# A hybrid encoder step on one core: the vector engine's part of a pair's first half is placed one slot behind the other engines' part

## What is computed

```python
h = rmsnorm(x, g_mix)
z = h @ w_in                                     # 1024 x 2048
ya, v_rows = gmlp_mix(gelu(z[..., :1024]), g_v, w_s, b_s)
xc, conv = causal_conv(z[..., 1024:1536], conv_buf, conv_w, conv_b)
yb, lru = rg_lru(xc, h0, w_a, b_a, w_i, b_i, lam)   # gates, then a scan over time
yb = yb * gelu(z[..., 1536:])
x = x + concat([rmsnorm(ya, g_out_a), rmsnorm(yb, g_out_b)]) @ w_out
# 8 heads x 16 experts for each token, out of 16384
q = rmsnorm(x, g_ffn) @ w_q
top-16 sums over two sets of 128 sub-keys -> expert numbers and softmax weights g
x = x + sum_k g_k * gelu(u_tab[e_k] . h2) * v_tab[e_k]
y = rmsnorm(x, g_final)
```

## Time and profile before

| | |
|---|---|
| median of 3 runs | 1813.78 us (1809.45 to 1820.84) |
| the profiled execution | 1812.19 us, its span 1810.4 us |
| busy share of the span: PE, DVE, ACT, POOL | 81%, 79%, 35%, 44% |
| mean granted clock of TensorE | 0.905 of full speed |
| chain that ended last, by engine | PE 31%, DMA 28%, DVE 16%, issue 9%, POOL 8%, ACT 7% |

### The profile page before, as it was taken

The page is one execution under the profiler, slowest core; times in us unless marked ns, Lnnn a source line. Parts: engine busy times, 40 slices in busy tenths (PEclk is TensorE's granted clock), DMA queues, the critical chain, the costliest instruction groups (busy, mean ns, idle before and its releaser), DMA issues.

```text
span 1810.4 us, 16904 instructions
## 1 busy us (share of the span) xinstructions
PE 1461.9 (81%) x4706; PEld 793.1 (44%) x4706; DVE 1426.9 (79%) x3039; ACT 634.1 (35%) x1935; POOL 796.1 (44%) x667
## 2 busy tenths in 40 slices
PE   6799796667675652876869988999998788899997
PEld 5485343433342212534735655433334455433332
DVE  1278688999898879689998999996668988766665
ACT  4335534232222221420147876221115666311112
POOL 2023234476777667758834444222223445322220
PEclk9899898877887786988979999999998988999999
DMA  9489999999999999989988989999998999999996
GB/s 351 155 332 409 388 354 385 339 399 412 394 400 408 384 415 403 389 313 403 380 308 319 357 331 379 417 417 417 417 417 340 375 343 348 409 417 417 417 417 254
DMA packets 146478, 675.75 MB, mean 373 GB/s; under 512 B 15216, under 2 KB 15472, under 8 KB 97232
## 3 DMA queue, kind: packets, MB, share of 16 engines
q0 software_dynamic: 92832, 538.39, 75.5%
q1 hardware_dynamic: 50496, 132.68, 19.0%
q10 hardware_dynamic: 3056, 3.61, 0.6%
HBM read 671.61 MB, written 3.01 MB: 373 GB/s over the span
## 4 chain that ended last, share of the span: by engine, by line
PE 31%; DMA 28%; DVE 16%; issue 9%; POOL 8%; ACT 7%; ACTq 0%; DVEq 0%; POOLq 0%; SPq 0%
DMA arena<-experts 19%; PE accY L1493 9%; DMA ring<-experts,idc 8%; PE pb L1478 8%; POOL ring L620 7%; PE pb L1298 4%; DVE ring L920 3%; DVE ring L909 3%; PE pb L1467 3%; PE pb L1307 2%; ACT arena L1223 2%; PE pq L1424 2%; DVE arena L969 1%; PE pb L1316 1%; POOL ring L618 1%
## 5 line engine op out<-in xcount | busy, mean ns | idle before, releaser
L618 POOL DMA_INDIRECT ring<-experts,idc x384 | 457.6, 1192 | 856.9 <-DVE xt L929 386.1
L909 DVE CUSTOM_DVE_ANT_0 ring<-ring,h 128x1024 f32<-128x1024 f32 x384 | 466.2, 1221 | 197.6 <-DMA ring<-experts,idc 196.4
L1493 PE MATMUL accY<-ring,diag 128*128 128x512 f32 x792 | 456.5, 713 | 200.4 <-ACT diag L1209 200.4
L1478 PE MATMUL pb<-arena 128*128 128x512 f32 x1024 | 473.6, 607 | 19.1 <-DMA arena<-experts 12.3
L620 POOL DMA_INDIRECT ring<-experts,idc x256 | 328.3, 1283 | 112.3 <-issue 76.9
L1198 ACT ACTIVATE ge<-zt 128x1 f32<-128x1 f32 x384 | 76.4, 199 | 771.6 <-DVE zt L909 770.4
L1493 PEld LDWEIGHTS accY<-ring,diag 128*128 128x128 f32 x792 | 161.5, 221 | 410.5 <-ACT diag L1209 271.9
L1478 PEld LDWEIGHTS pb<-arena 128*128 128x128 f32 x1024 | 186.2, 191 | 304.9 <-issue 195.0
L929 DVE SCALAR_TENSOR_TENSOR xt<-ring,coef,xt 128x1024 f32<-128x1024 f32 x186 | 238.1, 1280 | 7.5 <-ACT coef L1202 7.4
L1424 PE MATMUL pq<-arena 128*128 128x256 f32 (+1 forms) x768 | 152.5, 358 | 9.0 <-ACT arena L1193 4.7
L920 DVE CUSTOM_DVE_ANT_0 ring<-ring,arena 128x1024 f32<-128x1024 f32 x128 | 153.4, 1221 | 7.0 <-DMA ring<-experts,idc 6.1
(11 more groups left out here) (178 smaller groups left out, 1082.7 us busy)
## 6 DMA issues: line engine op xcount, KB each, us to landing
arena<-experts SPq DMA_DIRECT2D x128, 512.0 KB, 15.1
arena<-w_q SPq DMA_DIRECT2D x12, 2048.0 KB, 18.2
arena<-w_in SPq DMA_DIRECT2D x11, 2048.0 KB, 21.4
ring<-experts,idc POOLq DMA_INDIRECT x640, 9.3
arena<-w_out SPq DMA_DIRECT2D x4, 2048.0 KB, 20.7
ring<-w_out SPq DMA_DIRECT2D x2, 2048.0 KB, 20.3
xt<-x_all SPq DMA_DIRECT2D x5, 512.0 KB, 13.5
y_all<-xt ACTq DMA_DIRECT2D x5, 512.0 KB, 3.5
```

The costliest lines, as they stand in the source:

```text
L618: nc.gpsimd.indirect_dma_start(ring[:, at // 2], None, experts, index).then_inc(gat[at], 16)
L909: V.tensor_tensor_reduce(out=half(g), in0=half(g), in1=h2[:], scale=1.0, scalar=0.0, op0=ALU.mult, op1=ALU.add, accum_out=zt[:, s % 8:s % ...
L1478: ins = T.matmul(pb[:, 2 * j + k], cm[:, i, j * P:(j + 1) * P], vring[:, n % VRING, k * 512:(k + 1) * 512], start=i == 0, stop=i == BLOCKS ...
L1493: ins = T.matmul(accY[:, j], diag[:, (n - 1) % DIAGS], ring[:, place, D + j * 512:D + (j + 1) * 512], start=first, stop=final)
```

## The change

A second kind of item, `"Iv"`, stands for DVE's part of a step. It is due 1.2 us of the imagined schedule behind the step in the first pair and 0.8 us in the second; a step of the first pair is due every 2.2 us there, one of the second every 1.5 us. DVE acts on `"Iv"` in place of `"I"`; the other engines act on `"I"` as before. In the first tile's steps and in slots 0 to 3 of the first pair, `"Iv"` stands directly behind `"I"`. Weight loads and gathers are derived from the items that they were derived from before.

```diff
-    order = [("I", 0, p) for p in range(STEPS)]
+    order = [(kind, 0, p) for p in range(STEPS) for kind in ("I", "Iv")]
     for x in range(10):
         order.append(("II", 0, x))
         if x < 4:
             order.append(("I", 1, x))
+            order.append(("Iv", 1, x))
...
     for p in range(4, STEPS):
         put.append((1.06 + 2.2 * (p - 4), ("I", 1, p)))
+        put.append((1.06 + 2.2 * (p - 4) + 1.2, ("Iv", 1, p)))
...
     for p in range(STEPS):
         put.append((b + 4.03 + 1.5 * p, ("I", 2, p)))
+        put.append((b + 4.03 + 1.5 * p + 0.8, ("Iv", 2, p)))
...
             for item in ORDER:
-                if item[0] == "I":
+                if item[0] == "Iv":
                     front(item[1], item[2])
```

## The result

The changed kernel took 1807.5 us in the median of 10 runs (1801.87 to 1820.18), the kernel before 1817.03 us in the 10 runs beside them (1809.45 to 1824.93). The ratio is 0.9947, with a 95% interval of 0.9927 to 0.9968: 5.8 to 13.3 us less, about half a per cent. Measured again later, beside other kernels, it was 0.9975 (0.9955 to 0.9995). Both are inside 1%, so the change is small, and both are on the fast side of one.

What follows compares the result with a forecast made beforehand. No engine is full overall; DVE was taken to set the pace in the first pair's stretch, POOL in the second's. -5.7 - 2.4 = -8.1 us from 1812.19 gives 1804.1, 1805.7 by the median; forecast 1805, range 1794 to 1818.

Steps and rivals of the forecast that it cites:

- Steps 13 and 14: First pair: weighted adds now stand ahead; add 19 begins at 188.87, step 14 ends about 192.5, covered by step 16's wait.
- Step 16: First pair: dot 23 and a retrieval part fill its 8.33 us wait; step stays at 204.44, what follows 3.33 us sooner.
- Step 26: First pair: dot 42 and add 41 move ahead, so ACT's row mean starts 2.34 us sooner; PE's 2.05 us wait goes.
- Second pair: Beside the dense tiles' half-row gathers: dots fill DVE's waits, places free sooner, POOL's unbroken run starts 2.4 us earlier.
- The late start: Second pair, step 1: one dot now passes, so its reciprocal and what follows come 1.27 us late.
- The turn that closes the stretch: Sign of being right, end of second pair's stretch: the prepared numbers' turn comes some 8 us earlier than 923.68.
- The rule weighed: Second pair: dots in DVE's waits draw gathers out by 3.1 us, so the pair gains nothing; 1806.5 us, chance 0.07.
- the gain is absorbed: Rival, between the two pairs: a later wait is fixed by something else; 1812 us, chance 0.22.
- steps queue behind rows that have not landed: Rival, first pair's steps 23 to 26 and 28: moved steps wait with dots for rows; 1821 us, chance 0.11.
- the forecast's own sign of being wrong: First pair: DVE's waits for gathers grow beyond 12.3 us in total.
- POOL never waits: Rival, second pair: dots in DVE's waits keep every place free, 17.5 us go in place of 2.4; 1789 us, chance 0.10.

Runs made afterwards that it cites:

- the steps to 17: Against the kernel before, only the first pair's vector steps up to 17 are late, none of the second pair's; ratio 0.9981.
- A: Not a run: stretch from the third group of the first pair's input matmuls to POOL's first half-row gather; 208.62 us before the change.
- the one with step 26 alone: Against the kernel before, of all steps only step 26 of the first pair is late; ratio 0.9990.
- the two repeats: The changed kernel, and the one with only the first pair's steps late, each run again against the kernel before; ratios 0.9975 and 0.9976.
- full change: The changed kernel itself, vector steps of both pairs late, against the kernel before; 1807.5 us, ratio 0.9947.
- B: Not a run: stretch from ahead of the second pair's steps to the start of POOL's unbroken run of gathers; 140.36 us before the change.
- C: Not a run: part of B from the last dot ahead of step 1 in the old order (137th half-row dot) to B's end; 95.27 us before.
- the second pair alone: Against the kernel before, only the second pair's vector steps are late, the first pair's as before; ratio 0.9998.
- the first pair's run alone: Against the kernel before, only the first pair's vector steps are late, the second pair's as before; ratio 0.9962.
- with half of the bytes: First pair's steps late against the kernel before, tile 2's gathers bring quarter rows, dots multiplied by zero; 1816.52 us, ratio 1.0004. With both pairs late: 1811.46 us, 0.9982.
- the one with the first pair by 2.4: Against the kernel before, first pair's vector steps late by 2.4 in place of 1.2, second pair's as before; ratio 1.0037.
- the lag of 1.6: Full change, but second pair's steps up to 4 as before and its later ones late by 1.6 in place of 0.8; ratio to the kernel before 0.9961.

## Why the prediction came out as it did

The forecast's time and the sign were right: 8.1 us less were forecast, and the two ratios make it 9.6 and 4.5. In the first pair the mechanism holds, and part of the closeness is luck. The second pair's term is found in the profiles, where it had been priced, but can't be told in the times; and a part of the first pair's lead, which the forecast had kept whole, is lost between the pairs.

*Steps 13 and 14.* Right. Add 19 begins at 187.99 and step 14 ends at 191.5, for 188.87 and about 192.5. The add's wait of 4.96 us is the one that step 14's second product had there before (4.45 us), and the wait at step 16 covers the rest.

*Step 16.* Right in size: 2.49 us of wait left for 2.6. With the steps to 17, PE's wait ahead of the turn ends 4.2 us sooner, counted from the start of A (280.44 for 284.50), which is the 3.33 us priced and the 0.8 by which step 16 itself came sooner; 2.6 us of it are left at the queries, behind dots that wait longer for their rows. That PE goes from one matmul to the next up to 293 us but for two waits, which the forecast needed, rests on a stretch that the earlier trace rows leaves out (40.70 less 30.53 us are the 10.2 us idle):

```profile
252.30:293.00 40.70, 30.53 (x77) 14.15 (x76) 33.88 (x69) 14.96 (x41) 14.04 (x11) 0.87 0.97 384
```

One thing was missed. I had step 16 itself stay at 204.44; against the start of A it came 0.5 to 1.0 us sooner in eight profiles with the early steps of the first pair one slot late (203.55, 204.00 and 203.80 in the first three of them), and 0.3 in the one with step 26 alone. In the two repeats, where PE waited for the weight load, it came 0.1 and 1.1 us later. PE's wait ahead of the expert matmul at 161.05 us went from 2.14 to 1.50 us: a dot and a part of the retrieval run ahead of step 9 now, and ACT's scale for PE comes sooner. That this is the cause is read off the order, not tested.

*Step 26.* The sum came out; the term taken by itself was mis-sized. I priced it by the work moved ahead, 2.34 us, and said that ACT's row mean starts that much sooner. Alone it gained 1.55 us there and 0.17 at POOL: step 26 had 1.39 us of wait to fill and came late by the rest. Where the steps ahead of it moved too, its term was 1.8 us at the row mean and 2.0 in A. In the full change the row mean is 6.3 us sooner (270.09 for 276.39), where 5.7 had been forecast; step 16, which came 0.7 us sooner, is part of that. At the queries 4.85 us are left (300.47, where 299.6 was forecast), with more waits for rows ahead of them. That POOL's first half-row gather then comes 5.72 us sooner, for 5.7, is luck: 0.87 us of it is the granted clock in the queries, which was no part of the forecast. These first 32 queries took 7.07 to 7.43 us in most profiles with the first pair's single lag (8.24 in one), and 7.76 to 8.26 us in the three that leave the early steps in place, so it may come with the change; no run tests that.

*Second pair.* B does not show the 2.4 us: it is 140.7 to 141.1 in three of the four profiles with the lag, as before. Two things that stray with the lag as without hide it. Ahead of step 1 B strays: up to the 137th half-row dot, which stands there in every kernel, it took 43.3 to 47.2 us. And the input matmuls took 27.9 us or 29.5 to 30.9, with the lag as without. C leaves the first out, and compared between profiles whose inputs took as long it shows the term. At 27.9 us, C is 95.23 and 95.27 without the lag and 92.39 with it, 2.9 us less. At 29.5 to 30.9 us, it is 96.79 to 97.89 in four profiles without (97.3 in the mean) and 94.54 to 95.03 in three with it (94.9), 2.4 us less. These are few profiles, and the comparison was made after the runs, not foretold. The late start, which is in this sum, was one dot, as priced: 138 half-row dots run ahead of the reciprocal with the lag and 137 without. The waits that gave way are not quite those named: step 14's fell from 3.5 to 2.3 or 2.4 us, and those at steps 13 and 16 together are 11.8 to 12.8 us, for 12.6 to 14.0.

So the take of 2.4 us stands as far as the end of C. That it reaches the end of the kernel is not shown: the second pair alone gave 0.9998, with 0.9977 to 1.0020. The turn that closes the stretch was to come some 8 us earlier; it came 4.34 us earlier in the first profile of the full change, whose inputs took 3.0 us longer than those before.

*The rule weighed.* The forecast set the draw on gathers aside. POOL's half-row gathers were 1203 ns in the mean in the first pair's run alone, and with half of the bytes still 1407, at half of the DMA share. So neither the DMA engines nor the bytes draw them out. The Trainium skill's rule, on the page "SBUF — State Buffer", section "Who interferes with whom", names two-input vector work as what holds up a GpSimd instruction that reads SBUF. These runs agree in so far as the dots are what stayed the same. The price that the rival put on it, 3.1 us, did not come: the 81 gathers of B took 96.4 to 97.8 us of POOL together in five profiles without the second pair's lag (100.9 in the one with the first pair by 2.4), and 97.1 to 97.8 in the four with it. With the lag of 1.6 they took 100.2.

*The rivals.* That the gain is absorbed between the pairs came true in part. From POOL's first half-row gather to the gather at the start of B it took 322.9 to 323.1 us in the three profiles that leave the first pair's early steps in place (before, second pair only, step 26 alone), and 323.0 to 327.7, in the mean 325.2, in the ten with the single lag there (the two with quarter rows among them): some 2 us of the lead go. In the first profile of the full change it fell from 5.72 to 3.42 us. The times can't tell this from a lead that is kept: the two runs of the first pair alone gave 0.9962 and 0.9976, in the mean 5.6 us, each with an interval of 0.2% to either side. That steps queue behind rows that have not landed came in part too. Waits for rows grew from 12.3 to between 14.5 and 17.0 us in five profiles with the single lag, which was the forecast's own sign of being wrong, but A was shorter all the same; the sign was badly chosen. (The sum given with that rival was loose: five waits of 1.2 us use up the first pair's 5.7 us, not the whole 8.1.) That POOL never waits is wrong: from 762 to 801 us it still waited four times for 3 to 5 us.

## What to carry to other kernels

Putting other work ahead of one operation that waits gains at most the wait, so size the term by the wait in the timeline and not by the work moved; what is left over makes the operation late by that much. Where the operation before it moves too, the work taken from between them counts as well. Do it step by step: here an operation whose wait was long (8.33 us) could go back two slots, one that the next engine stands waiting for (the convolution ahead of the gate matmuls) made that engine wait 7.91 us when it went back two, and a uniform shift takes the bad with the good. To know where a gain of a few microseconds comes from, run the halves of the change by themselves, read them between two marks that lie close around the moved work, and compare profiles in which the matmuls of the stretch ran at the same granted clock.

## What the runs showed of the hardware

Fewer bytes in a gather did not make the stretch faster: the gathers with 2 KB a row took 1407 ns of POOL in the mean, those with 4 KB 1203, and the stretch was 16 us longer. That it would take longer was not expected, and no run explains it.

The 128 input matmuls of the second pair, the same instructions in every kernel, took between 27.86 and 30.87 us of PE in these profiles, with or without a lag, by when the granted clock rose. Two stretches before, and then three after the change, columns as in the earlier trace rows:

```profile
713.00:714.00 1.00, 0.32 (x2) 0.00 (x0) 1.00 (x3) 0.65 (x2) 0.69 (x2) 0.87 1.04 414
714.00:719.00 5.00, 4.03 (x19) 3.56 (x20) 5.00 (x9) 0.92 (x3) 4.09 (x4) 1.00 1.04 413
```

```profile
714.00:719.00 5.00, 5.00 (x12) 4.01 (x13) 5.00 (x9) 0.00 (x0) 4.39 (x3) 0.50 1.03 408
719.00:720.00 1.00, 1.00 (x4) 0.76 (x4) 0.50 (x2) 0.00 (x0) 0.69 (x2) 0.53 0.92 340
720.00:721.00 1.00, 1.00 (x6) 0.90 (x5) 0.94 (x1) 0.00 (x0) 0.70 (x2) 1.00 0.88 270
```

PE had stood idle for over 35 us and then began its turns, at 709.64 before and at 708.55 after. Before, it was granted full speed (2.4 GHz) by 714 us, ahead of the input matmuls; after the change it ran the first 6 us of them at half (1.2 GHz), 12 matmuls in 5 us where 19 went through in 4. The difference, 3.0 us, is larger than the second pair's whole forecast gain, and a reason not to read a single profile to the microsecond.
